# A fused two-block transformer kernel on one core: no zeroing products, earlier transposes of the memory, weight pieces rounded ahead, and a slot released without a drain

## What is computed

```python
def first_block(x, mem, ...):
    mem_n = rmsnorm(mem, mem_norm)
    h = x
    for layer in range(2):
        xn = rmsnorm(h, norm_mix[layer])
        if layer == 0:
            q, k, v, p = split(xn @ ev_w_in)                  # 4 x 512 columns
            mix = concat([moba_attention(q, k, v), multiscale_pool(p)]) @ ev_w_out
        else:
            mix = (spatial gating and gated delta rule of xn @ od_w_in) @ od_w_out
        h = h + mix
        h = h + memory_cross_attention(rmsnorm(h), mem_n, wq, wkv, wo)
        h = h + conv_ffn(rmsnorm(h), w_up, conv_w, w_down)
    return rmsnorm(h, final_norm)

def second_block(x, ...):
    for i in range(2):
        h = rms_norm(x)
        q_r, k_r, v_r, g_r, q_n, kv_n, gate_n, m_a, m_b = split(h @ w_in[i])
        y_ret = (silu(g_r) * normed(retention(q_r, k_r, v_r))) @ w_o_ret[i]
        kc, vc = compress(k_c), compress(v_c)                 # gelu(flat @ w1) @ w2
        y_nsa = nsa(q_n, kc, vc, k_s, v_s, k_w, v_w, sigmoid(gate_n)) @ w_o_nsa[i]
        x = x + (sigmoid(m_a) * y_ret + sigmoid(m_b) * y_nsa) @ w_out[i]
        x = x + (silu(a) * b) @ w_ffn_out[i]                  # a, b from rms_norm(x) @ w_ffn_in[i]
    return rms_norm(x, norm_final_g)
```

## Time and profile before

| | |
|---|---|
| time, median of 3 runs | 2014.54 us (2013.95 to 2016.91) |
| span of the profiled execution | 2013.8 us (the page gives no other time of it) |
| TensorE products busy | 1972.7 us (98%) |
| GpSimd busy | 1615.2 us (80%) |
| ScalarE busy | 1085.3 us (54%) |
| VectorE busy | 867.2 us (43%) |
| mean granted TensorE clock | 0.998 |

### The profile page before, as it was taken

How to read it: one execution, slowest core, us unless ns; L and a number is a source line. 1 busy time by engine, 2 the same in 40 slices (tenths; PEclk the granted TensorE clock), 3 DMA queues, 4 the chain that set the end, 5 groups by cost and what they waited for, 6 DMA issues and landing times.

```text
span 2013.8 us, 32648 instructions
## 1 busy us (share of the span) xinstructions
PE 1972.7 (98%) x12534; PEld 1716.0 (85%) x12534; DVE 867.2 (43%) x2052; ACT 1085.3 (54%) x2125; POOL 1615.2 (80%) x1272
## 2 busy tenths in 40 slices
PE   9999999999999999999999989999999999899998
PEld 8798999897798999898789768888987788678886
DVE  5512565067513565091414363562433322734641
ACT  4454666465354666444554775544444545865444
POOL 6785888987595888998798528999997897178997
PEclk9999999999999999999999999999999999999999
DMA  9853555553253675555456505555554467135552
GB/s 307 168 180 115 187 185 173 183 188 106 64 188 125 202 238 201 182 178 185 147 187 208 178 31 180 189 188 178 188 189 151 153 194 241 54 129 185 189 199 105
DMA packets 244272, 342.99 MB, mean 170 GB/s; under 512 B 8819, under 2 KB 172883, under 8 KB 243989
## 3 DMA queue, kind: packets, MB, share of 16 engines
q1 hardware_dynamic: 231832, 330.66, 49.6%
q10 hardware_dynamic: 12285, 10.24, 2.5%
HBM read 336.68 MB, written 4.19 MB: 169 GB/s over the span
## 4 chain that ended last, share of the span: by engine, by line
PE 90%; DVE 4%; ACT 3%; POOL 1%; issue 1%; DMA 1%; DVEq 0%; SPq 0%; POOLq 0%; ACTq 0%
PE bank L795 10%; PE bank L802 10%; PE bank L798 10%; PE bank L845 8%; PE bank L851 8%; PE bank L848 8%; PE bank L817 7%; PE bank L875 5%; PE bank L878 5%; PE bank L882 5%; PE bank L822 4%; DVE E L2351 1%; PE bank L1407 1%; DVE E L2337 1%; PE bank L763 1%; PE bank L1259 1%
## 5 line engine op out<-in xcount | busy, mean ns | idle before, releaser
L1616 POOL TENSOR_TENSOR w_lo<-ring,w_hi 128x512 fp32r<-128x512 f32 (+1 forms) x1216 | 1575.2, 1315 | 353.2 <-ACT w_hi L1714 315.5
L1714 ACT ACTIVATE w_hi<-ring 128x512 fp32r<-128x512 f32 (+1 forms) x1216 | 757.7, 630 | 769.3 <-PE bank L845 250.5
L795 PE MATMUL bank<-x_pair,w_hi 128*128 128x256 f32 x1504 | 379.5, 285 | 2.2 <-DVE x_pair L2237 1.4
L798 PE MATMUL bank<-x_pair,w_hi 128*128 128x256 f32 x1504 | 377.0, 283 | 0.0
L845 PE MATMUL bank<-w_hi,x_pair 128*128 128x512 f32 (+1 forms) x752 | 296.7, 395 | 5.4 <-ACT w_hi L1714 2.8
L795 PEld LDWEIGHTS bank<-x_pair,w_hi 128*128 128x128 f32 x1504 | 288.4, 192 | 4.9 <-issue 1.5
L848 PE MATMUL bank<-w_hi,x_pair 128*128 128x512 f32 (+1 forms) x752 | 290.6, 387 | 0.0
L798 PEld LDWEIGHTS bank<-x_pair,w_hi 128*128 128x128 f32 x1504 | 288.5, 192 | 0.4
L802 PE MATMUL bank<-x_pair,w_lo 128*128 128x256 f32 x1504 | 241.7, 283 | 0.0
L851 PE MATMUL bank<-w_lo,x_pair 128*128 128x512 f32 (+1 forms) x752 | 230.4, 388 | 2.7 <-POOL w_lo L1616 2.6
L802 PEld LDWEIGHTS bank<-x_pair,w_lo 128*128 128x128 f32 x1504 | 207.5, 192 | 0.0
(11 more groups left out here) (347 smaller groups left out, 2360.4 us busy)
## 6 DMA issues: line engine op xcount, KB each, us to landing
ring<-in_w_in SPq DMA_DIRECT2D x74, 1024.0 KB, 5.1
ring<-in_ffn_w_up SPq DMA_DIRECT2D x44, 1024.0 KB, 5.1
ring<-in_w_ffn_in SPq DMA_DIRECT2D x44, 1024.0 KB, 5.1
ring<-in_ffn_w_down SPq DMA_DIRECT2D x20, 1024.0 KB, 4.9
ring<-in_w_ffn_out SPq DMA_DIRECT2D x20, 1024.0 KB, 4.9
ring<-in_xattn_wkv SPq DMA_DIRECT2D x16, 1024.0 KB, 5.4
ring<-in_w_o_ret SPq DMA_DIRECT2D x16, 1024.0 KB, 4.9
ring<-in_od_w_in SPq DMA_DIRECT2D x12, 1024.0 KB, 5.1
```

The lines of the kernel that those rows point to most:

```text
L795: m = mm(out_, view(w_hi)[:, k, :], x_hi[:, 4 * kh + k, :], start=start, stop=False)
L798: mm(out_, view(w_hi)[:, k, :], x_lo[:, 4 * kh + k, :], start=False, stop=False)
L1616: tt(view(w_lo), src, view(w_hi), ALU.subtract).then_inc(w_lo_ready, 1)
L1714: return A(o, i_, ACT.Copy, **kw)
```

## The change

Four things change.

1. The zeroing products (L783) go: 16 of them, two in each of the eight units. The first product into each bank now starts it (c even, first half of x), and the second column tile of the bank opens without a start.
2. `turn_rows` moves ahead of the third piece of ev, and `turn_memory` ahead of its fifth. VectorE reads out the memory before ev. ScalarE rounds three pieces of ep before it waits for the table product.
3. `heads` on ScalarE takes the name of the unit that follows and rounds three pieces of it (HELD - 1) in its last step, ahead of the last pair's probabilities. This is done for 0mix0, 2onsa0 and 3onsa0.
4. The drain behind compression and its semaphore go. SyncE's queue waits instead for bank 6 to be full with the unit's products.

The diff:

```diff
--- before.py
+++ after.py
@@ -399,7 +399,6 @@
         full = [sem(f"bank_full{b}") for b in range(8)]
         empty = [sem(f"bank_empty{b}") for b in range(8)]
         landed = [[sem(f"half{j}_landed{s}") for j in range(2)] for s in range(RING)]
-        unit_read = sem("unit_read")
         w_hi_ready = sem("w_hi_ready")
         w_lo_ready = sem("w_lo_ready")
         piece_started = sem("piece_started")
@@ -580,16 +579,13 @@
             if name in BY_ROWS and "down" in name:
                 return 2 * min(4, FF_TILES - 4 * int(name[5:]))
             return PIECES
-        first_piece, whole_number = {}, {}
-        n_pieces = n_whole = 0
+        first_piece = {}
+        n_pieces = 0
         for name in order:
             if name in SPLIT:
                 assert n_pieces % HELD == 0
                 first_piece[name] = n_pieces
                 n_pieces += pieces(name)
-            else:
-                whole_number[name] = n_whole
-                n_whole += 1
 
         def wait_landed(eng, name, halves=(0, 1)):
             n = index[name]
@@ -779,8 +775,6 @@
                     open_bank = c % 2 == 0 and kh == 0
                     if open_bank:
                         B.take(pe, (name, c // 2), b)
-                    if open_bank and name in AFTER_NORM:
-                        mm(bank[b][:, :], nothing[:, 0:P], nothing[:, P:P + PIECE], start=True, stop=False)
                     if p == 2 and second_half:
                         second_half()
                     if p == PIECES - 1 and before_last:
@@ -791,7 +785,7 @@
                     for k in range(4):
                         if c == 0 and key:
                             x_ready(key, 4 * kh + k)
-                        start = kh == 0 and k == 0 and name not in AFTER_NORM
+                        start = kh == 0 and k == 0 and (c % 2 == 0 or name not in AFTER_NORM)
                         m = mm(out_, view(w_hi)[:, k, :], x_hi[:, 4 * kh + k, :], start=start, stop=False)
                         if k == 0:
                             m.then_inc(piece_started, 1)
@@ -883,10 +877,7 @@
                             if kt == tiles - 1:
                                 m.then_inc(full[b], 1)
 
-            def unit_done():
-                pe.drain().then_inc(unit_read, 1)
-
-            def channel_major(name, xT, tiles=4, width=512, finish=True, **kw):
+            def channel_major(name, xT, tiles=4, width=512, **kw):
 
 
                 if name in WIDE:
@@ -902,10 +893,8 @@
                             m = mm(bank[b0 + q][:, (c % 2) * SEQ:(c % 2 + 1) * SEQ], w[:, k, c * P:(c + 1) * P],
                                    xT[:, k, :], start=k == 0, stop=k == KT - 1)
                     m.then_inc(full[b0 + q], 1)
-                if finish:
-                    unit_done()
-
-            def token_major(name, xT, c0=0, n=512, width=512, finish=True, banks=None, **kw):
+
+            def token_major(name, xT, c0=0, n=512, width=512, banks=None, **kw):
 
                 if name in SPLIT:
                     return split_token_major(name, *xT, **kw)
@@ -1105,8 +1092,7 @@
             channel_major("eq", x_parts, key="0m", second_half=turn_x)
             spread_rstd("0m")
             channel_major("ek", x_parts)
-            token_major("ev", x_parts, after=turn_rows)
-            turn_memory()
+            token_major("ev", x_parts, second_half=turn_rows, after=turn_memory)
 
             pe.wait_ge(zero_ready, 1)
             pe.wait_ge(table_loads, 48)
@@ -1535,7 +1520,7 @@
                 if name in SPLIT:
                     sp.wait_ge(w_lo_ready, first_piece[name] + last_piece_of(name, j) + 1)
                 else:
-                    sp.wait_ge(unit_read, whole_number[name] + 1)
+                    B.wait_full(sp, ("hid", int(name[0]), "kv".index(name[-1])))
 
 
             def short(name):
@@ -1767,11 +1752,13 @@
                 high(key, (4, 5, 6, 7))
                 round_weights(name, 5)
 
-            def heads(hs, first=0):
+            def heads(hs, first=0, following=None):
                 n = len(hs)
                 for step in range(n + 2):
                     if first <= step - 1 < n:
                         exps(hs[step - 1])
+                    if step == n + 1 and following:
+                        round_weights(following, 0, HELD - 1)
                     if step >= 2:
                         probabilities(hs[step - 2])
 
@@ -1851,19 +1838,19 @@
                 for dst, src in later_rows[2 * p:2 * p + 2]:
                     act.dma_start(dst, src).then_inc(row_loads, 16)
             round_weights("ev")
+            round_weights("ep", 0, HELD - 1)
             B.wait_full(act, "table")
 
             copy(xs_table, bank[4][0:NSA_HEADS, 0:3 * P]).then_inc(empty[4], 1)
             B.wait_emptied(act, "table")
             act.dma_start(scratch.rearrange("q a x -> a q x"),
                           xs_table.unsqueeze(1).broadcast_to([NSA_HEADS, P, 3 * P])).then_inc(table_saved, 16)
-            round_weights("ep", 0, HELD)
-            round_weights("ep", HELD)
+            round_weights("ep", HELD - 1)
             for pair in causal_block1()[:EARLY]:
                 exps(pair)
-            heads(causal_block1(), first=EARLY)
-            for j in range(2):
-                round_weights(f"0mix{j}")
+            heads(causal_block1(), first=EARLY, following="0mix0")
+            round_weights("0mix0", HELD - 1)
+            round_weights("0mix1")
 
             def cross(L):
                 round_weights(f"{L}xkv0")
@@ -2152,8 +2139,8 @@
                 exps(nsa_heads(i)[1])
                 for t in range(TT):
                     evacuate((f"{L}mb1", "t", t), xs[:, t, 512:D], func=ACT.Copy, scale=rstd[:, t:t + 1])
-                heads(nsa_heads(i), first=EARLY)
-                round_weights(f"{L}onsa0")
+                heads(nsa_heads(i), first=EARLY, following=f"{L}onsa0")
+                round_weights(f"{L}onsa0", HELD - 1)
                 for t in range(TT):
                     m = A(xs[:, t, 512:D], xs[:, t, 512:D], ACT.Sigmoid)
                 m.then_inc(*NA.mark("gate"))
@@ -2430,10 +2417,6 @@
             tt(fold, fold, ident[:, 64:72], ALU.add)
             drain()
             tt(fold, fold, ident[:, 96:104], ALU.add)
-            for t in range(TT):
-                B.wait_full(dve, ("ev", "t", t))
-                b = B.uses[("ev", "t", t)][0]
-                ts(e_v[:, t, :], bank[b][:, :], rstd[:, t:t + 1], None, ALU.mult).then_inc(empty[b], 1)
             r0 = ROWS["mem_norm"][0]
             for t in range(TT):
                 for q in range(2):
@@ -2441,6 +2424,10 @@
                     b = 4 + 2 * t + q
                     tt(memT[:, 4 * q:4 * q + 4, t * P:(t + 1) * P], bank[b][:, :].rearrange("p (a b) -> p a b", a=4),
                        spread(vecs[:, r0 + 4 * q:r0 + 4 * q + 4], P), ALU.mult).then_inc(empty[b], 1)
+            for t in range(TT):
+                B.wait_full(dve, ("ev", "t", t))
+                b = B.uses[("ev", "t", t)][0]
+                ts(e_v[:, t, :], bank[b][:, :], rstd[:, t:t + 1], None, ALU.mult).then_inc(empty[b], 1)
             B.wait_full(dve, "cmpbias")
             parts_of = bank[5][:, 0:len(CMP_TILES) * 2 * NSA_HEADS].rearrange("p (b s c) -> p b s c", s=2, c=NSA_HEADS)
             places = [(cmpbias[:, 0, 0:CMP_SEEN, :], parts_of[:, 0:CMP_SEEN]),
```

## The result

| | before | after |
|---|---|---|
| median of 20 runs each | 2015.37 us (2013.95 to 2017.72) | 2018.90 us (2014.98 to 2022.79) |
| ratio, 95% interval | | 1.0014 (1.0008 to 1.0020) |
| profiled execution: time, span | span 2013.8 | 2017.26, span 2015.5 |
| mean granted clock of that execution | 0.998 | 0.997 |

The change makes the kernel slower by 0.14% (the medians lie 3.5 us apart), inside the 0.2% that count as no change here but on the other side of the forecast, and the time lies above the range.

A forecast was written before the change was run, and what follows sets the result against it. TensorE's own work, 90% of the span, was taken as the bound. The terms -3.2 (zeroing), -1.2 (drains), -2.1 (early transposes), +0.3 (layer 0) and +4.2 (held VectorE) gave -2.0: 2014.5 to 2012.5 us, range 2008.0 to 2016.5.

The forecast's parts named there:

- third rival: Ends of heads, layers 2 and 3: clock falls behind the lengthened wait, up to 1.7 us each, 2015.9 us; chance 0.25.
- main case: Whole kernel: the forecast sum of -2.0 us, giving 2012.5 us; chance 0.27.
- I take the fall of the clock as gone: Behind ev: early transposes put full products in the quiet stretch and end the low clock, -1.7 us, bounds 0 and 1.7.
- Held VectorE: Heads' end, layers 2 and 3: GpSimd's earlier remainders hold two of VectorE's four operations, +2.1 us each, +4.2 together.
- No gain from the roundings ahead: Ends of heads, layers 0, 2 and 3: no wait for w_hi or w_lo found, so nothing to win.
- Layer 0: End of layer 0's heads: three roundings delay the last probabilities and TensorE's last values wait, +0.3 us.
- Drains: Behind compression: four drains at 0.37 us, 1.5 in all, less 0.3 returning; taken as -1.2 us, bounds 0.5 and 1.5.
- The wait that was to return at mb0: Layer 2, mb0: slack 0.43 us against 0.74 from two drains, so 0.3 us comes back as a wait for w_lo.
- zeroing products: All units: sixteen products of 0.24 us go, -3.2 us, with 0.1 each behind three down-projections; bounds 2.9 and 3.8.
- The table's wait: Behind ev: the table's wait for bank 4, 0.21 us by the row, 0.4 start to start, goes: -0.4 us.
- The rule against the early rows: VectorE's vector work beside GpSimd's remainders of ev: one or two of seven operations held; all held gives 2015.1, chance 0.05.
- the row and the page differ: Early vector work: L2421 took 0.17 us unhindered beside GpSimd, though the skill page says such two-input operations contend.

The follow-up runs named there:

- roundings-ahead kernel: The kernel before with only the third part, weight pieces rounded ahead of the last probabilities: 2022.99 us, ratio 1.0036.
- wait filled: The changed kernel with 12 unused 512-column products on TensorE in the wait ahead of the heads' last transposes, layers 2 and 3: 2015.89 us, ratio 1.0001.
- turns alone: The kernel before with only the early transposes in ev, ep's early rounding and VectorE's copies behind the memory: 2014.76 us, ratio 0.9994.
- GpSimd waiting: The changed kernel with GpSimd's remainders in layers 2 and 3 waiting until VectorE has finished the last pair: 2011.63 us, ratio 0.998.
- the four ahead of the table: The kernel before with four unused 512-column products between the memory's transposes and the table: 2016.22 us, ratio 1.0002.
- fillers among the small products: The kernel before with an unused 512-column product behind every second of the 15 products of 32 columns: 2020.71 us, ratio 1.0024.

## Why the prediction was wrong

**The step that failed is the treatment of the clock, at two places.** Against the third rival the forecast said that no row had an idle time of 3 us and that one of 1.09 had left the clock alone. That was absence of evidence. The forecast had itself lengthened the wait to 3.2 us (3.13 measured), and gave the case in which the clock then falls only a quarter, less than its own main case. In place of the 0 that the sum had for the clock at the heads, the rows show +1.56 and +1.57 us. The change's profile has the fall at both places, the roundings-ahead kernel at one of two, and with the wait filled it is at neither. Medians put it at 3.0 us for the two.

The other place is "I take the fall of the clock as gone", -1.7. It was read from one execution. In that of the change it was indeed gone, but by the spans so it is in about a third of the runs of before and half of those with the turns alone. Two of the kernels with the early transposes (GpSimd waiting, wait filled) have it in their profiles. The term should have been near 0; a median already holds such a fall at its own rate. The forecast named both doubts ("one profile can't show"), and then took the full gain.

It also took it off the wrong number. The profiled span of before looked 0.7 us under the median, but time is span plus 1.8, so that execution took 2015.6 us, 1.1 over the median of the three first runs. That median, 2014.54, is a span of 2012.7, where the runs without the fall lie: there was no fall in it to win back.

With these two set right, by the forecast's own terms, 2012.5 + 1.7 + 3.4 = 2017.6, against a median of 2018.9. Another 0.8 is the base: the median of before is 2015.37 over 20 runs.

**Right or nearly so:**
- Held VectorE: two operations per layer, forecast 2.1 each, measured 2.17 and 2.10, and by the kernels without it and with GpSimd waiting shown to be GpSimd's early start. The two that were held took 1.29 and 1.37 us each. The Trainium skill ("SBUF — State Buffer", section "Who interferes with whom") counts `tensor_scalar` among the operations that can take the port pair shared with GpSimd, and has the later comer wait for a whole instruction. The trace agrees: 3.04 us in place of 1.01, one GpSimd instruction (3.83 / 3 = 1.28 us) for each held operation.
- No gain from the roundings ahead in any of the three series: with the hold taken away they leave 2011.63 beside 2011.13 without them.
- Layer 0: +0.3 forecast, +0.27 measured.
- Drains: 0.36, 0.34, 0.36 and 0.33, forecast 0.37 each. The wait that was to return at mb0 did not show in the change's profile. It did with the drains alone and in variants of the change, and with the drains alone it took back about 0.65 us, not 0.3.

**A little off:** zeroing products, forecast -3.2, measured -2.7 (2.9 by the medians of the part alone). The 0.1 us that was to come through at each of the three down-projections did not. The wait for x hid all of the 0.24, and the up-projections' first ones were worth 0.2 rather than 0.24. The table's wait was 0.25 rather than 0.4.

**The rule against the early rows** did not change the time, but the forecast read its row wrongly. L2421, called unhindered at 0.17 us, ran from 40.66 to 40.83. It ended 0.03 us behind the end of a GpSimd instruction (40.80), and the next one began at 40.89. So it could not show that such an operation is never held. In the change's profile the same operation (L2408) takes 0.39 us, and L2414, also of two inputs from SBUF, 1.16:

```profile
37.95 0.39 DVE L2408 TENSOR_TENSOR g_both<-vecs 128x8 f32<-128x8 f32 x1
38.53 1.25 DVE L2412 CAST nothing<-rel 33x16 fp32r<-33x16 f32 x1
39.86 1.16 DVE L2414 TENSOR_TENSOR nothing<-rel,nothing 33x16 fp32r<-33x16 f32 x1
41.49 0.69 DVE L2425 TENSOR_TENSOR region<-bank,vecs 128x512 f32<-128x512 f32 x1
```

All three of the first rows end within 0.03 us behind the end of a GpSimd instruction (38.31, 39.76 and 40.99). So the forecast's "the row and the page differ" does not stand, and three of the seven are held, not one or two. VectorE still comes to the memory at 41.49, long before the table at 47.12.

## What to carry to other kernels

Work that is moved ahead of a critical operation on one engine also moves what that work sets off on the others. Follow it to the next engine, and where GpSimd would start beside the small VectorE operations that TensorE waits for, let GpSimd wait for them (that took the whole hold away). An idle time of TensorE that grows to 3 us should be priced with a fall of the clock behind it, here 1.6 us on top in three of four places, and its price can be measured by filling it with unused products. A stretch at low clock in one profile is one sample: look at the spread of the runs before counting it as won, and see whether the run that the forecast starts from had it.

## What the runs showed of the hardware

- The same wait, 3.13 and 3.14 us of idle TensorE behind the same instructions, was followed by a fall of 3.4 us (1.6 lost), by none at all, and in one case by a low clock of 6.8 us (2.6 lost). The Trainium skill ("TensorE: Matmul & The Clock Gate", section "What's actually happening") says that the phase of the clock gate's monitor is not tied to the program, so that one kernel differs from run to run. The rows agree so far: the wait was the same and what followed was not. That the phase is the reason no run here shows.
- A stretch of the program in which TensorE is hardly idle (0.2 us), only busy with small products and transposes, had the same fall behind it, by the spans in half of the runs or more: 9 products in 3.3 us where the kernel with GpSimd waiting had it, against 16 in 3.4 where the clock was whole.
- A full product between products of 33 rows and 32 columns costs 0.53 us of TensorE, where in a stream of its kind it takes 0.23 at the full clock (the four ahead of the table start that far apart).
- The spans of a kernel's runs stand in groups about one fall apart. A comparison of medians between such kernels mixes work gained with the number of falls. The lowest groups separate them, but only among runs taken side by side: that of before stood at 2012.1 to 2012.6 beside the first four kernels and at 2012.7 to 2013.4 beside the next. Beside the first it was 2007.5 to 2008.4 without roundings ahead, about 4.4 us lower, where the parts give 2.7 + 1.4 + 0.25.
- The low clock behind ev lasted 6.8 us in place of 3.4 in two of the profiles, with the drains alone and with fillers among the small products.
